# A different order of slots within an expert block of a mixture-of-experts step

## The chip, the cores and the metric

The kernel runs on one core of a Trainium2 chip. The metric is the device time of one execution in microseconds (us); the median of several runs is given. One further execution was recorded by the hardware profiler, and all rows shown below are of that one.

## The reference

One decoder layer is computed for 1040 prompt tokens (16 of them learned meta tokens) and 8 sample tokens, 1048 rows of 1024 numbers in float32: a mixer, then a mixture of experts, then a last norm. The mixer is not touched here. The mixture of experts is, cut to what matters:

```python
lg = h2 @ rg_w + rg_b;  gsel = top_k(lg, 1)            # one of 4 groups
le_g = (h2 @ re_w + re_b) of the chosen group          # 8 experts
ev, ei = top_k(le_g, 2)                                # two of the 8
wts = softmax(lg)[gsel] * softmax(ev)
for e in range(32):
    he = silu(h2 @ w_gate[e]) * (h2 @ w_up[e])         # 1024 -> 256
    out += combine[:, e] * (he @ w_down[e])            # 256 -> 1024
```

Each token is thus a row of two of the 32 experts, and 1048 x 2 = 2096 rows are to be worked on. The chosen experts depend on the data.

## The kernel before, in words

**Stages.** The mixer comes first. From about 500 us on, `route_parts` multiplies the mixer's result by the output weights (L2045) tile by tile (nine tiles of 128 tokens), and computes the router's choice of each tile on VectorE. From about 620 us on the expert stage runs, and from about 990 us on the last norm, which reads the experts' results back.

**How rows come to slots.** An expert has a block of C = 128 slots; one slot is one partition of the block's tile. In `place(t)` each token's *rank* within its expert is known: the number of tokens before it with the same expert. A token goes to the slot c for which `ic[c]` equals its rank:

```python
tt(in_slot[:, :, :], bc(rank[:, :, t], C), bc1(ic[:, :], 2), ALU.is_equal)
```

The product of this 0/1 matrix with the token numbers (`tabulate`, L1997) yields a table with a source row, a target row and a weight for each slot and expert. Slots without a token hold a row number out of bounds. `ic` is a constant of 128 columns, the same in each partition, that GpSimd writes with an iota in the function `gpsimd` (L1678). It counts 0, 1, 2, ..., so that the first n slots of a block with n tokens are filled. Ranks of 128 and more go to further blocks, at most 16 (`vector_extra`, L1931, compares with the same `ic`); here there are two such blocks.

**The expert stage.** Block e is worked on in these steps. GpSimd gathers the rows of the table from memory to the tile `xg`, 4 KB to a partition, with an indirect DMA (`gather`, L2088); rows out of bounds are left out. TensorE turns the tile (L2209). ScalarE and VectorE split the weights and the rows in a high and a low part (L2242, L2247, L2324, L2328), and TensorE makes three products of them for gate and up (L2273; two of the eight parts of the contraction, L2277, are made plain) and for down (L2349). VectorE and ScalarE weigh the result into `out`, and GpSimd scatters it with a second indirect DMA (L2200) to memory. Blocks 0 and 1 and the further blocks take plain products (L2256, L2315).

**Order.** TensorE does, for each block j: turn block j+2, turn the gated rows of j, gate and up of j+1, down of j. Three tiles and three sets of weights are in rotation. SyncE's queue loads the weights of block j+3: half of gate and up (L2110, 640 KB each of `w_gate` and `w_up`, both on one semaphore) when block j's first half is used, the other half (384 KB each) after the second, and down (L2127, 1024 KB) after block j's down products. The gather of block j+3 is issued when block j has been turned. All 128 slots are computed, filled or not.

Of the kernel before, what the change touches and what calls it, by code (L numbers as in the profile page):

```python
# [33 lines left out]
C = 128  # L34
# [1487 lines left out]
def route_parts(nc, m, s, b, io, sample):  # L1522
# [31 lines left out]
    ic = m.place("r_ic", [P, C])  # L1554
# [23 lines left out]
    part, base, isov = (m.place("r_" + name, [P, 2, T]) for name in ("part", "base", "isov"))  # L1578
# [27 lines left out]
    def h2_stored(eng):  # L1606
        eng.wait_ge(h2_out[0], 16 * 5)
        eng.wait_ge(h2_out[1], 16 * 4)
# [63 lines left out]
    def gpsimd(pool):  # L1672
        pool.wait_ge(b.ya_out[0], 16 * 2)
        it = nc.gpsimd.iota
        kw = dict(allow_small_or_imprecise_dtypes=True)
        it(iw[:, :], pattern=[[-1, 8]], base=8, channel_multiplier=0, **kw)  # L1676
        it(ib[:, :], pattern=[[1, OV]], base=1, channel_multiplier=0, **kw)
        it(ic[:, :], pattern=[[1, C]], base=0, channel_multiplier=0, **kw)  # L1678
        it(thr[:, :], pattern=[[C, PARTS - 1]], base=C, channel_multiplier=0, **kw)
        for k in range(2):  # L1680
            it(vals[:, 0, k, :], pattern=[[-P, T]], base=NOWHERE, channel_multiplier=-1, **kw)
            it(vals[:, 1, k, :], pattern=[[-P, T]], base=NOWHERE - k * TOK, channel_multiplier=-1, **kw)
        nc.gpsimd.memset(cum[0][:, :], 0.0).then_inc(iota, 1)
        sample.scale(pool)
        pool.wait_ge(prod, T)
        for k in range(SLOTS):
            nc.gpsimd.memset(b.xg[k][:, :], 0.0).then_inc(iota, 1)
        pool.wait_ge(iota, SLOTS + 1)
        h2_stored(pool)
        pool.wait_ge(b.rows_ok, 1)  # L1690
        for k in range(SLOTS):
            gather(pool, b, k, k)
# [385 lines left out]

    f = Shared()
    f.sync, f.gpsimd, f.scalar, f.vector, f.tensor, f.sync_more = sync, gpsimd, scalar, vector, tensor, sync_more  # L2080
    f.vector_extra, f.vector_tables, f.tensor_extra = vector_extra, vector_tables, tensor_extra
    f.idle_products, f.totals = idle_products, totals
# [3 lines left out]
def gather(pool, b, k, e, done=None):  # L2086

    pool.indirect_dma_start(b.xg[k][:, :], None, b.h2_dram,  # L2088
                            bass.IndirectOffsetOnAxis(ap=b.slot_rows[:, 0, e:e + 1].bitcast(U32), axis=0),
                            bounds_check=TOK - 1, oob_is_err=False).then_inc(b.gathered[k] if done is None else done, 16)  # L2090
# [767 lines left out]
```

## Time and profile before

| | |
|---|---|
| median of 3 runs | 1040.01 us (1036.04 to 1042.16) |
| the profiled execution | 1034.48 us, span 1032.7 us |
| TensorE busy | 974.1 us, 94% of the span |
| VectorE, ScalarE, GpSimd busy | 672.7, 503.6, 149.5 us |
| moved by DMA | 220.90 MB, of it 17.19 MB on GpSimd's queue |

The time of a run is a little longer than the span, which goes from the first to the last instruction. Busy shares are means over stages that differ; the chain of work that ended last tells what set the time of each stage. The share of the DMA engines is the time that packets took on the 16 engines of the core.

### The profile page before, as it was taken

The numbers are of one execution on the slowest core, as the hardware profiler recorded it, in microseconds if no ns is written. First come the engines' busy times: TensorE is split into PE (matmuls) and PEld (weight loads), VectorE is DVE, ScalarE is ACT, GpSimd is POOL, SyncE is SP. The second block draws the span as 40 slices with busy tenths as digits, with TensorE's granted clock in tenths as the row PEclk, the third lists the DMA queues.
The fourth block names the chain that finished last, engine by engine and source line by source line (L and its number), as shares of the span: only waits on it lengthen the run. The fifth ranks groups of instructions, "written<-read, shape, count | busy, mean of one in ns | idle before, by whom it ended". The sixth has DMA issues, their size and how long they took to land.

```text
span 1032.7 us, 15104 instructions
## 1 busy us (share of the span) xinstructions
PE 974.1 (94%) x5448; PEld 828.5 (80%) x5448; DVE 672.7 (65%) x1041; ACT 503.6 (49%) x891; POOL 149.5 (14%) x114
## 2 busy tenths in 40 slices
PE   5999999998999999999999988999999999999855
PEld 4889999998999999998888865677777777776422
DVE  7457676697434635356666667688887878787117
ACT  7487776433222332333223222577776766665115
POOL 2000000000000000000300011234434344442000
PEclk9999999999999999999999999999999999999988
DMA  7114667425753565458221159999999999995557
GB/s 243 45 42 126 164 156 198 119 83 170 207 157 109 155 167 135 142 166 264 79 82 59 48 225 294 375 356 372 379 367 349 354 346 360 347 393 213 187 212 313
DMA packets 127820, 220.90 MB, mean 214 GB/s; under 512 B 69516, under 2 KB 82374, under 8 KB 127758
## 3 DMA queue, kind: packets, MB, share of 16 engines
q1 hardware_dynamic: 115554, 194.20, 57.1%
q0 software_dynamic: 9792, 17.19, 4.5%
q10 hardware_dynamic: 2412, 8.68, 2.1%
q8 instruction: 38, 0.62, 0.2%
q14 instruction: 24, 0.20, 0.1%
HBM read 191.79 MB, written 46.72 MB: 231 GB/s over the span
## 4 chain that ended last, share of the span: by engine, by line
PE 75%; DMA 9%; DVE 9%; ACT 4%; issue 2%; SPq 0%; ACTq 0%; DVEq 0%; POOLq 0%
PE psum L1141 27%; PE psum L2045 10%; PE psum L2273 8%; DMA wd<-w_down 8%; PE psum L2349 5%; PE psum L2277 3%; PE psum L2256 2%; PE psum L1164 1%; PE psum L2209 1%; PE psum L2315 1%; PE psum L1980 1%; DVE it L953 1%; DVE xi L955 1%; ACT wd_hi L2324 1%; PE psum L1246 1%
## 5 line engine op out<-in xcount | busy, mean ns | idle before, releaser
L1141 PE MATMUL psum<-hh,wh 128*128 128x350 f32 x672 | 223.4, 332 | 3.9 <-issue 3.9
L1141 PE MATMUL psum<-hh,wl 128*128 128x350 f32 x672 | 217.9, 324 | 0.0
L1141 PE MATMUL psum<-hl,wh 128*128 128x350 f32 x672 | 217.3, 323 | 0.0
L1141 PEld LDWEIGHTS psum<-hh,wh 128*128 128x128 f32 x672 | 127.8, 190 | 5.3 <-issue 4.1
L1141 PEld LDWEIGHTS psum<-hl,wh 128*128 128x128 f32 x672 | 127.4, 190 | 0.9
L1141 PEld LDWEIGHTS psum<-hh,wl 128*128 128x128 f32 x672 | 127.2, 189 | 0.0
L2247 DVE TENSOR_TENSOR wgu_lo<-wgu,wgu_hi 128x1536 fp32r<-128x1536 f32 x60 | 104.9, 1749 | 0.5 <-ACT wgu_hi L2242 0.4
L2328 DVE TENSOR_TENSOR wd_lo<-wd,wd_hi 128x2048 fp32r<-128x2048 f32 x30 | 68.8, 2292 | 35.1 <-ACT wd_hi L2324 34.8
L2242 ACT ACTIVATE wgu_hi<-wgu 128x1536 fp32r<-128x1536 f32 x60 | 89.2, 1489 | 0.0
L2200 POOL DMA_INDIRECT expert_rows<-out,slot_rows x34 | 54.2, 1595 | 218.7 <-DVE out L2367 213.5
L2273 PE MATMUL psum<-wgu_hi,xgt_hi 128*128 128x512 f32 x180 | 85.3, 474 | 0.2
L2088 POOL DMA_INDIRECT xg<-h_rows,slot_rows x34 | 76.3, 2244 | 31.7 <-issue 17.6
L2324 ACT ACTIVATE wd_hi<-wd 128x2048 fp32r<-128x2048 f32 x30 | 57.6, 1918 | 41.2 <-DMA wd<-w_down 41.2
L855 DVE TENSOR_TENSOR wl<-wst,wh 128x1024 fp32r<-128x1024 f32 x28 | 34.3, 1225 | 64.4 <-ACT wh L629 64.3
L2273 PE MATMUL psum<-wgu_hi,xgt_lo 128*128 128x512 f32 x180 | 70.8, 394 | 0.0
L2273 PE MATMUL psum<-wgu_lo,xgt_hi 128*128 128x512 f32 x180 | 70.6, 392 | 0.0
L1676 POOL IOTA r_iw<- 128x8 f32 x1 | 0.1, 143 | 414.4 <-DMA mixer_rows<-th 414.4
L2277 PE MATMUL psum<-wgu,xgt_rest 128*128 128x512 f32 x120 | 56.3, 592 | 0.0
L897 DVE SCALAR_TENSOR_TENSOR acc<-raw,cqw,acc 128x1072 f32<-128x1072 f32 x36 | 48.0, 1333 | 0.9
L2045 PE MATMUL psum<-wo_hi,yt_hi 128*128 128x512 f32 (+1 forms) x144 | 47.8, 413 | 0.0
L2045 PE MATMUL psum<-wo_lo,yt_hi 128*128 128x512 f32 (+1 forms) x144 | 44.9, 393 | 0.0
L2273 PEld LDWEIGHTS psum<-wgu_hi,xgt_hi 128*128 128x128 f32 x180 | 33.9, 188 | 13.6 <-issue 8.0
(350 smaller groups left out, 1842.8 us busy)
## 6 DMA issues: line engine op xcount, KB each, us to landing
wd<-w_down SPq DMA_DIRECT2D x34, 1024.0 KB, 14.7
wgu<-w_gate SPq DMA_DIRECT2D x34, 640.0 KB, 6.0
wgu<-w_up SPq DMA_DIRECT2D x34, 640.0 KB, 13.4
wst<-w_in SPq DMA_DIRECT2D x28, 512.0 KB, 4.0
wgu<-w_gate SPq DMA_DIRECT2D x34, 384.0 KB, 6.5
wgu<-w_up SPq DMA_DIRECT2D x34, 384.0 KB, 14.6
ck<-qkv_rows SPq DMA_DIRECT2D x9, 702.0 KB
qkv_rows<-acc SPq DMA_DIRECT2D x12, 520.0 KB, 6.1
```

What stands on the lines that cost most here:

```text
L897: stt(ac[:, 0:QLEN], rw[:, q:q + QLEN], w[:, q:q + 1], ac[:, 0:QLEN], ALU.mult, ALU.add).then_inc(taps if q < KQ - 1 else conv_ok, 1)
L1141: ins = mm(ps[:, c, 0:ZC], w[:, kk, :], a[:, kk, c * ZC:(c + 1) * ZC], start=(kk == 0 and q == 0), stop=(kk == KD - 1 and q == 2))
L2045: ins = mm(ps[0:n, 2 * (t % 2) + c, :], y, w[:, c * 512:c * 512 + 512], start=(i == 0 and q == 0), stop=(i == KD - 1 and q == 2))
L2088: pool.indirect_dma_start(b.xg[k][:, :], None, b.h2_dram, bass.IndirectOffsetOnAxis(ap=b.slot_rows[:, 0, e:e + 1].bitcast(U32), axis=0), b ...
L2200: pool.indirect_dma_start(b.ye, bass.IndirectOffsetOnAxis(ap=b.slot_rows[:, 1, e:e + 1].bitcast(U32), axis=0), out[p][:, :], None, bounds_ ...
L2242: nc.scalar.activation(w_hi[x.p][h][:, :, :, :], half_of(b.slots[x.k][0], h), ACT.Copy).then_inc(w_hi_ok[h][x.p].sem, 1)
L2247: nc.vector.tensor_tensor(half_of(b.slots[x.k][1], h), half_of(b.slots[x.k][0], h), w_hi[x.p][h][:, :, :, :].bitcast(F32), ALU.subtract).t ...
L2273: ins = nc.tensor.matmul(gate_up_bank(x.p), a[:, c, :], w, start=(c == 0 and i == 0), stop=(c == KP - 1 and i == 2))
L2277: ins = nc.tensor.matmul(gate_up_bank(x.p), xt_rest[x.p][:, c, :], raw[:, :, kk, :], start=False, stop=False)
L2324: nc.scalar.activation(wd_hi[x.p][:, :, :], b.slots[x.k][2][:, :, :], ACT.Copy).then_inc(wd_hi_ok[x.p].sem, 1)
L2328: nc.vector.tensor_tensor(b.slots[x.k][3][:, :, :], b.slots[x.k][2][:, :, :], wd_hi[x.p][:, :, :].bitcast(F32), ALU.subtract).then_inc(wd_ ...
L2349: ins = nc.tensor.matmul(ps[0:C, 4 + 2 * x.p + c, :], h[x.p][:, f, :], w[:, f, c * 512:c * 512 + 512], start=(f == 0 and i == 0), stop=(f ...
```

## The change

The constant `ic` is written by four iotas of 32 columns each in place of one of 128. The column c = 32k + 4a + b, with k from 0 to 3, a from 0 to 7 and b from 0 to 3, gets the value 16 (k mod 2) + floor(k / 2) + 2a + 32b. This is a permutation of 0 to 127. The tokens of an expert thus go to other slots: rank 0 to slot 0, rank 1 to slot 64, rank 2 to slot 4, rank 32 to slot 1. The table, the gathers and the scatters follow from it, since they only use the table.

```diff
         it(iw[:, :], pattern=[[-1, 8]], base=8, channel_multiplier=0, **kw)
         it(ib[:, :], pattern=[[1, OV]], base=1, channel_multiplier=0, **kw)
-        it(ic[:, :], pattern=[[1, C]], base=0, channel_multiplier=0, **kw)
+
+        for k in range(4):
+            it(ic[:, 32 * k:32 * k + 32], pattern=[[2, 8], [32, 4]], base=16 * (k % 2) + k // 2, channel_multiplier=0, **kw)
         it(thr[:, :], pattern=[[C, PARTS - 1]], base=C, channel_multiplier=0, **kw)
```

## Rows read from the trace of the kernel before

**Rows 1.** The page: busy time of TensorE; queues with packets, MB, engines' share

```profile
PE 974.1 (94%) x5448; PEld 828.5 (80%) x5448; DVE 672.7 (65%) x1041; ACT 503.6 (49%) x891; POOL 149.5 (14%) x114
...
q1 hardware_dynamic: 115554, 194.20, 57.1%
q0 software_dynamic: 9792, 17.19, 4.5%
```

**Rows 2.** The chain that ended last, 560 to 1033 us: start, length, what

```profile
671.83 2.77 PE psum L2349 x12
...
779.24 2.77 PE psum L2349 x12
...
789.61 2.79 PE psum L2349 x12
792.56 15.98 DMA wd<-w_down
...
951.95 2.77 PE psum L2349 x12
...
969.56 7.15 PE psum L2256 x16
...
987.08 2.57 DMA expert_rows<-out,slot_rows
```

**Rows 3.** ScalarE's waits, 654 to 957 us: total, times, longest

```profile
ACT wd_hi L2324 <- DMA wd<-w_down: 41.2, 20, 2.9
```

**Rows 4.** Busy time by stretch; last three columns: TensorE clock, DMA share, GB/s

```profile
654.00:784.00 130.00, 129.87 (x582) 98.47 (x581) 109.17 (x105) 92.81 (x108) 50.74 (x26) 1.00 0.98 365
...
790.00:924.00 134.00, 131.60 (x583) 99.69 (x582) 108.93 (x105) 92.80 (x106) 55.05 (x26) 1.00 0.97 358
...
610.00:616.00 6.00, 3.04 (x23) 2.74 (x23) 4.62 (x24) 4.28 (x19) 0.00 (x0) 0.94 1.02 414
645.00:650.00 5.00, 5.00 (x34) 3.91 (x33) 0.84 (x2) 2.95 (x3) 0.00 (x0) 1.00 1.02 421
964.00:967.00 3.00, 3.00 (x8) 1.33 (x7) 0.00 (x0) 0.00 (x0) 0.00 (x0) 1.00 1.03 420
```

**Rows 5.** DMA issues, 654 to 674 us: KB each, median us to landing

```profile
wd<-w_down SPq DMA_DIRECT2D x2, 1024.0 KB, 7.2
wgu<-w_gate SPq DMA_DIRECT2D x2, 640.0 KB, 6.2
wgu<-w_up SPq DMA_DIRECT2D x2, 640.0 KB, 7.8
```

**Rows 6.** DMA issues, 774 to 794 us

```profile
wd<-w_down SPq DMA_DIRECT2D x2, 1024.0 KB, 16.1
wgu<-w_gate SPq DMA_DIRECT2D x2, 640.0 KB, 5.9
wgu<-w_up SPq DMA_DIRECT2D x2, 640.0 KB, 14.6
```

**Rows 7.** DMA issues, 955 to 984 us

```profile
wgu<-w_gate SPq DMA_DIRECT2D x1, 640.0 KB, 4.8
wgu<-w_up SPq DMA_DIRECT2D x1, 640.0 KB, 6.8
```

**Rows 8.** GpSimd in order of time, 423 to 504 us: start, length

```profile
423.00 0.24 POOL L1678 IOTA r_ic<- 128x128 f32 x1
423.19 0.14 POOL L1679 IOTA r_thr<- 128x8 f32 x1
423.28 0.15 POOL L1681 IOTA r_vals<- 128x9 f32 x1
...
503.70 1.61 POOL L1443 TENSOR_TENSOR s_in<-s_in,vals 128x512 f32<-128x512 f32 x1 [79.95 <-PE psum L1480]
```

**Rows 9.** VectorE in order of time, its first step of the router

```profile
491.53 0.25 DVE L1809 SCALAR_TENSOR_TENSOR lg<-psum,stat,rb 128x36 f32<-128x36 f32 x1 [6.63 <-PE psum L1980]
```

## The prediction

> **What bounds the kernel now.** I read the page first, then the chain of work that ended last over the last 480 us, then the waits in the expert stage, then the busy and transfer rates of single stretches, and last the DMA issues stretch by stretch. The page says TensorE is busy 94% of the span, and that two queues matter for this change: q1, which carries the weights, and q0, GpSimd's, which carries the gathers and scatters [rows 1]. The edit touches only which partition a row takes in the gathers and scatters, so the stage to understand is the expert stage, from about 654 to 954 us.
>
> Its chain has two parts. The rows of the chain at L2349 are the down products, one for each block. From 671.83 (block 2) to 779.24 (block 13) there are twelve of them in 11 equal steps, and nothing but TensorE stands between them: 107.41 / 11 = 9.765 us a block. That is TensorE's own pace. The next comes 10.37 us later, and from there to 951.95 (block 30) the chain runs again and again through a piece of about 16 us of "DMA wd<-w_down" [rows 2]. From block 13 to block 30 the 17 steps take 951.95 - 779.24 = 172.71 us, so 10.16 us each, where TensorE's pace would give 17 x 9.765 = 166.0. So the weights hold the second half of the stage up by 6.7 us. The waits agree on the place: ScalarE waits 41.2 us in 20 pieces for the down weights before it splits them, and most of that is slack of ScalarE itself, of which 6.7 us reach TensorE [rows 3].
>
> Why are the weights late? One block needs 3072 KB of weights (1024 down, 2 x 640 and 2 x 384 gate and up), which is 3.146 MB, and 17.19 MB / 34 = 0.506 MB of gathered and scattered rows [rows 1]: 3.65 MB in 9.765 us is 374 GB/s. The stage gets 365 GB/s in its first part and 358 in its second, with the DMA engines shown as 98% and 97% busy. Yet in three stretches in which nearly nothing but weights moved, the same engines gave 414, 421 and 420 GB/s [rows 4]. So 358 is no limit of the memory for such reads, and something in the mix makes full-looking engines slow.
>
> The issues of single stretches show what. The gate and the up half-load of 640 KB are issued one right after the other and count up the same semaphore. In 654 to 674 the first reaches its count after 6.2 us and the second after 7.8. In 774 to 794 the first takes 5.9 us, as ever, and the second 14.6; the down load has gone from 7.2 to 16.1 us [rows 5, 6]. Two transfers of one size in one queue can't land 9 us apart if all engines are equally far. But the two together make 32 counts, one for each engine and load, and "the first" is only the first 16 of them. If half of the engines are on time and have done both loads by 6 us, and the other half lags by 9 us, these are exactly the numbers. At the end of the stage, in the blocks of rows beyond 128, the pair lands after 4.8 and 6.8 us, so the same pair can be close [rows 7].
>
> And half the engines is what the kernel would load. 1048 tokens x 2 choices over 32 experts are 65.5 rows a block, and ranks are given to partitions in order from 0, so nearly all rows lie in partitions 0 to 63. An engine that serves a fixed group of partitions gets twice its share in the lower half and nearly nothing in the upper one. The sizes fit: 3.146 / 16 + 0.506 / 8 = 0.260 MB on an engine of the loaded half, over 10.16 us, is 25.6 GB/s, and 420 / 16 = 26.2 GB/s is what an engine does with weights alone [rows 1, 2, 4]. The lag is consistent too: from 7.2 to 16.1 us in 120 us, or 12.3 blocks, is 0.7 us a block, so that the loaded half needs some 10.2 to 10.5 us a block against TensorE's 9.765; after about a dozen blocks the three buffers' lead is used up, and that is where the chain changes [rows 2, 5, 6].
>
> The Trainium skill says the same of the place (DMA: Bandwidth & Descriptors, "The descriptor swizzle"): in a 128-partition transfer an engine serves eight fixed partitions, with bit 6 and bits 2 to 4 of the partition number choosing it, which puts partitions 0 to 63 on eight engines; after the change any 16 ranks in a row would by it fall on 16 engines. No row names an engine, so here that stays the skill's; what the rows show is that half of the counts lag.
>
> **The change part by part.** *The iota.* One IOTA of 128 columns (0.24 us) goes and four of 32 columns come. The short ones around it, of 8 to 16 columns, take 0.14 to 0.15 us, the long one 0.24, so four lie between 0.56 and 0.96 us busy, and the net cost on GpSimd is +0.3 to +0.7 us at 423 us. Behind them stand the other constants; the one who waits for these is VectorE, whose first use is at 491.53, 68 us later and after a wait for TensorE, and GpSimd itself then idles 79.95 us [rows 8, 9]. Cost 0; without that cover it would be at most 0.7 us.
>
> *The comparison with ic* (L1862, L1931) has the same shape with other values: 0. The products that build the table, the transposes, gate, up and down products work on all 128 rows in any case: 0.
>
> *The gathers and scatters.* The number of instructions, of rows, and of refused indices stays. What moves is the partition. Columns 32k+4a+b get rank 16(k mod 2) + floor(k/2) + 2a + 32b. So ranks 0 to 31 fill every fourth partition, 0 to 63 two of every four. Whatever fixed group of at least four neighbouring partitions an engine serves, it gets nearly the same number of rows. The load of each engine becomes 3.65 / 16 = 0.228 MB a block. At 26.2 GB/s that is 8.7 us, at the 25.6 worked out above 8.9; both lie 0.85 us or more under TensorE's 9.765. Then no backlog grows, the down load lands some 5 to 8 us after its issue instead of 16, the wait of 41.2 us at L2324 is gone, and the stage keeps TensorE's pace to its end. What is late next is TensorE itself, so nothing more than the 6.7 us can be had here.
>
> *Bounds.* Above: 6.7 us saved in full. Below: none, if the rows cost the engines their time wherever they lie: weights at 420 GB/s take 7.49 us, which leaves 10.16 - 7.49 = 2.67 us for 0.506 MB, or 190 GB/s [rows 2, 4]. Half of the engines, or slow rows on all: the sum alone can't tell the two apart, only the counts that split in two halves can [rows 6]. I take the full 6.7 for that reason.
>
> *Before and behind the stage.* The first gathers come sooner by perhaps 1 us, but the way to block 0's gated rows leads through VectorE's tables. The products of the last extra block start at 969.56, when the ones before end; they keep their distance. The last scatter takes 2.57 us, nearly all of it fixed [rows 2]: at most 0.5 us less, taken as 0.
>
> Here a rule of the skill speaks against the change. The Trainium skill (SBUF — State Buffer, "A bandwidth-pool intuition that's wrong (but worth ruling out)") puts the path from HBM to a core at about 358 GB/s and calls it nearly always the end-to-end bottleneck. By it a block's 3.65 MB need 10.2 us, spread or not, and the time would stay at 1040.0. The second half of the stage runs at 358, in its favour, but the rows with 414 to 421 GB/s are against it.
>
> **Sum.** -6.7 + 0 + 0 = -6.7 us. The profiled execution took 1034.48 us with a span of 1032.7; it would become 1027.8. The median of the runs is 1040.01 (1036.04 to 1042.16), 5.5 us above the profiled one; the same step there gives 1033.3, or 0.64% less. About 0.5%, 5.2 us, is what a measurement of this kernel can tell from no change.
>
> **The rivals.**
> *A common limit.* Reads, gathers and scatters share some 358 to 375 GB/s whatever the engines, or small rows are slow in themselves. For: 190 GB/s for the rows, above. Against: the halves of the counts that drift apart. Gain 0, so 1040.0; a mixture that leaves the period at 9.95 gives 17 x 0.2 = 3.4 us, 1036.6. Chance 0.21, nearly all of it within 0.5%. The skill's 358 GB/s, above, is this rival.
> *Rows dealt out to engines one by one* (partition modulo 16) and not by groups: this is the one that ends slower. Before, each engine would have its even share; after, ranks below 64 lie in partitions 0 and 1 of every four, which are 8 of 16 engines. Each of these would get 0.506 / 16 = 0.032 MB more, 1.2 us a block, and the period would be 10.16 + 1.2 = 11.4. From block 2 on, after a lead of some 6 us: 29 x (11.4 - 9.765) - 6 - 6.7 = 35 us more, about 1075. It decides from the point where the loaded engines need more than now. Against: with even shares now, no half of the counts could be early. Chance 0.03.
> *TensorE's clock.* With no pauses left TensorE is busy all through the stage, and the chip might grant less. In 654 to 784 it is busy 129.87 of 130 us, at a granted clock of 1.00, which is 2.4 GHz [rows 4], so full business there has not brought the lower level. If it came for 10 us, the stage would lose 5: 1038. Chance 0.04.
> *The edit has no effect on engines* (they take shares by the order of the descriptors that have data): 1040.0; counted with the common limit.
>
> **How the numbers follow.** The forecast has 0.70, with an own range of 1030.5 to 1036 from the spread of a median of few runs; the two rivals without a gain 0.25 together, the slower one 0.03, and 0.02 for more gain than I see. Of the forecast's 0.70 about 0.60 come out beyond 0.5%, since 6.7 us is close to 5.2; with the last 0.02 faster is 0.62. Within 0.5%: 0.10 + 0.21 + 0.02 = 0.33. Slower: 0.05. The range takes in the case without a gain: 1028.5 to 1040.
>
> **What would show it.** Right: L2349 in the chain steps by 9.77 us to block 30, at about 945.2 for that row instead of 951.95; no "DMA wd" pieces of 16 us in it; the wait at L2324 under 5 us; gate and up of a pair landing within 2 to 3 us of each other in every stretch; the down load at 5 to 8 us; some 370 GB/s at 90% DMA share. Wrong: pairs that still drift apart, or landings together but still at 12 us or more, would be the common limit. A granted clock under 1.00 between 654 and 950 would be the third rival.

## The result and the profile after

The changed kernel took 1032.34 us in the median of 7 runs (1028.33 to 1036.81), the kernel before 1037.29 us in 7 runs (1035.27 to 1042.16). The ratio is 0.9938, with a 95% interval of 0.9915 to 0.9961: 0.6% faster. (The two medians alone lie 4.95 us apart, 0.5%.) The profiled execution after took 1032.16 us, with a span of 1030.4 against 1032.7.

The chain of work that ended last, 560 to 1033 us (start, length, what). The lines of the code have moved by two, so L2351 is the L2349 of before:

```profile
676.55 2.77 PE psum L2351 x12
...
783.96 2.77 PE psum L2351 x12
...
793.72 2.77 PE psum L2351 x12
...
940.22 2.77 PE psum L2351 x12
...
949.10 2.79 PE psum L2351 x12
954.51 12.98 DMA wd<-w_down
...
985.05 2.34 DMA expert_rows<-out,slot_rows
```

From block 2 (676.55) to block 29 (940.22) lie 27 steps of 9.766 us without one exception, and no piece of waiting for weights stands between them; before, such pieces of 16 us began at 792 [rows 2]. From block 2 to block 30 the stage takes 949.10 - 676.55 = 272.55 us, before 951.95 - 671.83 = 280.12: 7.6 us less.

Busy time by stretch (last three columns: TensorE clock, DMA share, GB/s), then the DMA issues of 774 to 794 us (KB each, us to landing), then ScalarE's longest waits in 654 to 957 us:

```profile
654.00:784.00 130.00, 130.00 (x581) 97.92 (x580) 108.73 (x105) 89.86 (x104) 50.77 (x26) 1.00 0.99 364
790.00:924.00 134.00, 134.00 (x604) 102.85 (x603) 114.14 (x111) 95.25 (x109) 53.51 (x28) 1.00 1.01 373
```

```profile
wd<-w_down SPq DMA_DIRECT2D x2, 1024.0 KB, 9.3
wgu<-w_gate SPq DMA_DIRECT2D x2, 640.0 KB, 5.9
wgu<-w_up SPq DMA_DIRECT2D x2, 640.0 KB, 7.9
```

```profile
ACT thx L2286 <- PE psum L2275: 48.5, 30, 3.3
...
ACT out L2362 <- PE psum L2351: 37.9, 30, 3.6
```

TensorE is busy in all of the 134 us from 790 to 924, where it was 131.60 [rows 4]. The gate and the up load land 2.0 us apart, where it was 8.7 [rows 6]. ScalarE's wait for the down weights, 41.2 us before [rows 3], has no row any more; ScalarE now waits for TensorE.

The profile as a whole is only 2.3 us shorter, though. The iotas on GpSimd, which wait for a mixer result, start at 426.36 us after and at 422.81 before: 3.5 us are lost before the first changed instruction. From there to block 2 it is 250.19 against 249.02, 1.2 more. The stage gives 7.6, the tail takes 0.8 (from block 30's down products to the last scatter 35.95 us, before 35.13), and the end gives 0.3. What stands ahead of the iotas can't be the change's doing; the rows show where the two executions part there. The stretches of before, and then of after (the third last column is TensorE's granted clock):

```profile
52.00:78.00 26.00, 23.43 (x141) 21.64 (x141) 14.25 (x23) 22.13 (x37) 0.00 (x0) 1.00 0.12 41
640.00:660.00 20.00, 20.00 (x85) 12.68 (x84) 8.14 (x11) 8.35 (x9) 2.71 (x2) 0.94 1.00 401
```

```profile
52.00:78.00 26.00, 23.43 (x126) 20.96 (x125) 13.79 (x22) 18.87 (x32) 0.00 (x0) 0.87 0.07 21
640.00:660.00 20.00, 18.17 (x71) 10.93 (x72) 6.37 (x14) 4.60 (x7) 0.00 (x0) 0.83 0.97 382
```

From 52 to 78 us TensorE was granted 0.87 of full speed after and 1.00 before, and 26 x 0.13 = 3.4 us is nearly all of the 3.5. From 640 to 660 us it was 0.83 against 0.94, which is enough for the 1.2. Such stretches differ between executions of one kernel: from 52 to 78 us the change was granted 0.87 in two profiles and 0.93 in a third (again2), as was in_order. So the medians, and not the two profiles, are the measure of the change.

### The profile page after: what moved, and what is told of

Its sections match the earlier page's. It is cut to its first block, busy times and chain, and to the rows that moved or that the text cites. A ratio compares the mean times of both kernels' runs of the same rounds, so it can differ in the third digit from the quotient of the medians.

```text
span 1030.4 us, 15107 instructions
## 1 busy us (share of the span) xinstructions
PE 975.8 (95%) x5448; PEld 832.6 (81%) x5448; DVE 674.7 (65%) x1041; ACT 502.1 (49%) x891; POOL 141.4 (14%) x117
## 3 DMA queue, kind: packets, MB, share of 16 engines
q0 software_dynamic: 9792, 17.19, 4.8%
## 4 chain that ended last, share of the span: by engine, by line
PE 85%; DVE 8%; DMA 3%; ACT 2%; issue 1%; SPq 0%; DVEq 0%; ACTq 0%; POOLq 0%
PE psum L1141 27%; PE psum L2275 12%; PE psum L2047 10%; PE psum L2351 8%; PE psum L2279 5%; PE psum L2211 3%; PE psum L1164 2%; PE psum L2258 2%; PE psum L1982 1%; PE psum L2317 1%; DMA wd<-w_down 1%; DVE it L953 1%; DVE xi L955 1%; PE psum L1246 1%; DVE acc L897 1%
## 5 line engine op out<-in xcount | busy, mean ns | idle before, releaser
L2090 POOL DMA_INDIRECT xg<-h_rows,slot_rows x34 | 67.6, 1988 | 32.0 <-PE psum L2211 11.5
L2369 DVE TENSOR_SCALAR out<-psum,slot_w 128x512 f32<-128x512 f32 x34 | 25.5, 751 | 52.5 <-PE psum L2351 42.7
L2286 ACT ACTIVATE thx<-psum 128x256 f32<-128x256 f32 x34 | 13.1, 384 | 76.6 <-PE psum L2275 48.5
```

Of the source, the lines that this page charges most:

```text
L2090: pool.indirect_dma_start(b.xg[k][:, :], None, b.h2_dram, bass.IndirectOffsetOnAxis(ap=b.slot_rows[:, 0, e:e + 1].bitcast(U32), axis=0), b ...
```

## The experiments

All ratios are to runs of the kernel before on the same chip, with 95% intervals.

**The change once more, and its slots undone.** The first is the kernel after as it is.

> The change once more, beside the next three on one chip. All theories: some 6 us (0.6%) below the kernel before, no 16 us piece of waiting for the down weights in the chain, gate and up of a pair landing some 2 us apart.

The second keeps the four iotas and gives back the old values:

```diff
-            it(ic[:, 32 * k:32 * k + 32], pattern=[[2, 8], [32, 4]], base=16 * (k % 2) + k // 2, ...)
+            it(ic[:, 32 * k:32 * k + 32], pattern=[[4, 8], [1, 4]], base=32 * k, ...)
```

> Four iotas as in the change, but with the values 0 to 127 in order, so the slots are those of before. My theory (the partitions of the rows count, the iotas are hidden): same time as before, ratio 0.998 to 1.002, the up load lands 14 to 15 us after its issue in the second half of the stage. Rival (something about the program itself, such as a different alignment of code or clock, made the gain): ratio near 0.994.

Measured: 0.989 (0.9867 to 0.9912) for the change, and 0.9988 (0.9967 to 1.0008) in order. In order, the up load lands after 14.7 us in 790 to 924, gate after 6.0, ScalarE waits 40.8 us for the down weights (654 to 957 us), and block 2 to block 30 takes 953.67 - 673.81 = 279.86 us. All the gain is in the order of the slots.

**Which partitions count?** Two other permutations part the ways in which an engine could be tied to partitions. In the first, ranks 0 to 63 fill the partitions whose bit 2 is 0; in the second, those whose bit 5 is 0.

```diff
+            it(ic[...], pattern=[[2, 4], [64, 2], [16, 4]], base=8 * (k % 2) + k // 2, ...)   # bit2_last
+            it(ic[...], pattern=[[2, 8], [16, 4]], base=64 * (k % 2) + k // 2, ...)           # bit5_last
```

> Ranks 0 to 63 in the partitions whose bit 2 is 0 (0 to 3, 8 to 11, ...), spread evenly over every run of eight neighbouring partitions and over both halves. If an engine serves two groups of four partitions chosen by bits 2 to 4 and 6, as the Trainium skill has it, eight engines again get nearly all rows: ratio 0.998 to 1.002, up load at 14 us, 16 us waits in the chain. If an engine serves eight neighbouring partitions, or if it is enough that the rows lie over all 128 partitions: even load, ratio near 0.994, up load near 8 us.

> Ranks 0 to 63 in the partitions whose bit 5 is 0 (0 to 31 and 64 to 95), the other half of the partitions nearly empty. If bits 2 to 4 and 6 choose the engine, all 16 engines have the same number of rows as with the change: ratio near 0.994, up load near 8 us. If an engine serves eight neighbouring partitions, or if all 128 partitions must be used: ratio 0.998 to 1.002, up load at 14 us.

DMA issues of 790 to 924 us, with bit 2 last, and then with bit 5 last:

```profile
wd<-w_down SPq DMA_DIRECT2D x13, 1024.0 KB, 15.4
wgu<-w_gate SPq DMA_DIRECT2D x14, 640.0 KB, 6.2
wgu<-w_up SPq DMA_DIRECT2D x14, 640.0 KB, 13.8
```

```profile
wd<-w_down SPq DMA_DIRECT2D x13, 1024.0 KB, 9.0
wgu<-w_gate SPq DMA_DIRECT2D x14, 640.0 KB, 6.0
wgu<-w_up SPq DMA_DIRECT2D x14, 640.0 KB, 8.0
```

With bit 5 last half of the partitions are nearly empty, and yet the pair lands 2.0 us apart, the stage takes 272.54 us (677.26 to 949.80), and the ratio is 0.9901 (0.9878 to 0.9924), that of the change. With bit 2 last the rows lie in all parts of the 128 partitions, 4 in every 8, and yet the pair drifts 7.6 us apart, and the waits for down weights are back: 41.3 us at ScalarE, and pieces like this one in the chain (900 to 1000 us):

```profile
914.80 2.79 PE psum L2350 x12
917.60 16.93 DMA wd<-w_down
...
945.95 2.77 PE psum L2350 x12
...
954.82 2.79 PE psum L2350 x12
```

So neither "it is enough that all 128 partitions are used" nor "an engine serves eight neighbours" holds. The runs speak for four of the seven bits: with ranks 0 to 63 on one value of bit 6 (slots in order) or of bit 2 the pair drifts apart, with one value of bit 5 or of bit 1 (the change, whose ranks 0 to 63 lie in partitions with bit 1 at 0) it does not. Bits 0, 3 and 4 were not parted. All this agrees with the Trainium skill's rule (DMA: Bandwidth & Descriptors, "The descriptor swizzle"): bit 6 and bits 2 to 4 choose the engine, and bit 5 and bits 0 and 1 do not. The profile has no engine numbers, so the rule is seen here by its effect alone.

One number missed its expectation. With bit 2 last the ratio is 0.9937 (0.9914 to 0.996) and not 1.00. The stage takes 278.05 us (676.77 to 954.82), 2 less than before. That accounts for 0.2% of the 0.6%; the rest was not found in the stage (see what stays open). As to the 2 us: eight engines carry most rows in both kernels, but not equally. By that rule and the routing of these inputs, worked out with the reference, the fullest engine has 7.6 rows a block and transfer with the slots in order (the one of partitions 0 to 3 and 32 to 35 is full in every block of 36 tokens or more) and 6.9 with bit 2 last. The next experiment measures this.

**The transfers laid bare.** In the kernel itself TensorE's pace hides most of what the transfers need. So a third of the gate and up products of the split parts is left out, and with it VectorE's subtraction that feeds it, while every transfer stays:

```diff
-                for i, (a, w) in enumerate(((hi_x, hi_w), (hi_x, lo_w), (lo_x, hi_w))):
+                for i, (a, w) in enumerate(((hi_x, hi_w), (hi_x, lo_w))):
...
-                if x.parts:
-                    turned_low(dve, x)
+                pass
```

The waits for the result of that subtraction go with it.

> Slots as before, but TensorE's third product of gate and up (low rows by high weights) is left out, and with it VectorE's subtraction that makes the low rows; all transfers stay. TensorE then needs some 7.4 us a block, VectorE 7.3, so that the transfers alone set the pace from early on. Skewed engines: 10.1 to 10.2 us a block, the time within 5 us of the kernel before, although a quarter of TensorE's work is gone. If the 10.16 us of the kernel before came from an interplay with TensorE, the block would get faster.

> The same cut with the slots of the change. Skewed engines: the load of the fullest engine falls from some 0.259 to 0.233 MB a block, so 9.0 to 9.2 us a block, and 25 us or more less than light_before. Common limit (all transfers share one rate wherever the rows lie): the same pace as light_before, 10.1 us a block.

> The same cut with ranks 0 to 63 in the partitions whose bit 2 is 0. By the fullest engine (6.9 rows a block and transfer instead of 7.6 before, worked out from the routing): 0.254 MB, 9.9 to 10.0 us a block, some 4 to 6 us below light_before and 20 above light_after. If only the split in halves counted: as light_before.

ScalarE's split of the down weights comes once a block, so its rows in order of time (start, length) give the pace. Two rows of each kernel, 19 blocks apart: slots in order, those of the change, bit 2 last.

```profile
693.46 1.92 ACT L2323 ACTIVATE wd_hi<-wd 128x2048 fp32r<-128x2048 f32 x1 [2.10 <-DMA wd<-w_down]
...
890.12 1.92 ACT L2323 ACTIVATE wd_hi<-wd 128x2048 fp32r<-128x2048 f32 x1 [3.22 <-DMA wd<-w_down]
```

```profile
697.30 1.92 ACT L2325 ACTIVATE wd_hi<-wd 128x2048 fp32r<-128x2048 f32 x1
...
862.71 1.92 ACT L2325 ACTIVATE wd_hi<-wd 128x2048 fp32r<-128x2048 f32 x1 [0.89 <-DMA wd<-w_down]
```

```profile
692.55 1.92 ACT L2324 ACTIVATE wd_hi<-wd 128x2048 fp32r<-128x2048 f32 x1 [2.59 <-DMA wd<-w_down]
...
881.31 1.92 ACT L2324 ACTIVATE wd_hi<-wd 128x2048 fp32r<-128x2048 f32 x1 [2.58 <-DMA wd<-w_down]
```

| slots | us a block | median, us | ratio | fullest engine by the rule, MB a block |
|---|---|---|---|---|
| in order | 196.66 / 19 = 10.35 | 1035.74 | 0.997 (0.9941 to 0.9999) | 0.197 + 2 x 7.6 x 0.0041 = 0.259 |
| bit 2 last | 188.76 / 19 = 9.93 | 1029.63 | 0.992 (0.9896 to 0.9944) | 0.253 |
| the change's | 165.41 / 19 = 8.71 | 998.82 | 0.9618 (0.9574 to 0.9662) | 0.233 |

The weights alone are 3.146 / 16 = 0.197 MB on an engine, and 0.0041 MB is a row. The change's slots have 4.5 rows for the 7.6 and take 0.197 + 2 x 4.5 x 0.0041 = 0.233.

With the slots in order TensorE's smaller work brings 3 us; the blocks don't get faster with less for TensorE to do (10.35 us here, and (951.95 - 789.61) / 16 = 10.15 in the kernel before [rows 2]), so the transfers and not an interplay with TensorE set that pace. With the change's slots the same cut brings some 33 us. TensorE alone would need 8.36 us there, as the next experiment shows, and the 19 steps hold one of 8.36 us before ScalarE's waits begin, so that 8.71 (8.73 without that step) is an upper bound of what the transfers need. And these transfers, rows and all, run at this rate (stretches of light_after):

```profile
700.00:760.00 60.00, 59.17 (x263) 44.12 (x262) 51.38 (x49) 47.86 (x55) 25.61 (x15) 1.00 1.03 417
780.00:880.00 100.00, 99.40 (x441) 74.03 (x440) 86.63 (x84) 80.40 (x93) 43.22 (x24) 1.00 1.03 415
```

415 GB/s with gathers and scatters in it is the rate that weights alone had before (414 to 421) [rows 4]. The common limit of 358 GB/s is refuted, and so are rows that are slow in themselves. The order of the three follows the fullest engine: the eight loaded engines carry nearly the same mean in the first two lines (6.6 and 6.7 rows by the same count), but the pace differs by 0.4 us. The rates by the table (0.259 / 10.35 = 25.0 GB/s, 25.5, 26.8) don't agree to better than 7%, so the fullest engine alone is a good guide and no exact law. Two expectations were missed: 8.71 us is below the 9.0 to 9.2 that I gave light_after, and light_bit2 is 31 us above light_after and not 20. A third premise was wrong too: the cut takes 9.77 - 8.36 = 1.4 us of TensorE's block, 14% and not a quarter.

**Fewer bytes in place of a better order.** In `gather`, `bounds_check` is 0 in place of TOK - 1, so that every row but row 0 is left out and the experts work on zeros (the results are not those of the layer), once on the light kernel with the change's slots, once on the kernel before.

> light_after, and the gathers take no rows: their bound is 0, so every index above 0 is left out and the experts work on zeros; instructions, indices and scatters stay. By bytes on even engines: 0.215 MB, 8.4 us a block, 0.6 to 0.8 us below light_after. If a gathered row costs the engines much more than its bytes (row reads slow in themselves, 2.67 us a block for gathers and scatters together), it is 1.3 us or more below light_after.

This one told nothing of what it was for. Its blocks take (853.33 - 694.49) / 19 = 8.36 us with TensorE busy 100.00 of 100 us, so TensorE, which I had put at 7.4 us, set the pace, and the transfers lay below it. It gives an upper bound only, and a ratio of 0.9528 (0.9483 to 0.9574).

> Slots as before, full TensorE work, but the gathers take no rows (bound 0; the experts work on zeros, the scatters stay). The fullest engine's load falls from some 0.259 to 0.228 MB a block, under TensorE's 9.77 us at 25.5 GB/s. If the bytes on the fullest engine set the pace before: all steps of the stage at 9.77 us and the ratio of the change, 0.989 to 0.994, with the skewed slots. If the order of slots did something else: the ratio stays at 0.998 to 1.002.

Ratio 0.9914 (0.9887 to 0.9941). The chain of this kernel, with the slots in order:

```profile
672.93 2.77 PE psum L2349 x12
...
936.60 2.77 PE psum L2349 x12
945.47 2.79 PE psum L2349 x12
```

Block 2 to block 30 takes 272.54 us, to 0.01 the time of the change. Taking the gathered bytes off the loaded engines does as much as spreading them; both only bring the transfers under TensorE's pace.

**The tail, and the change a third time.** In the profile after, TensorE has a new wait in the blocks of rows beyond 128 (TensorE in order of time, 955 to 972 us; the window cuts the 16 products to 11):

```profile
967.53 4.99 PE L2258 MATMUL psum<-wgu,xgt 128*128 128x512 f32 x11 [0.79 <-DMA wd<-w_down]
```

There gate, up and down loads count up one semaphore, and gate and up wait for all. `tail_split` gives the down load its own:

```diff
+    more_d = s.again_pair("v_d")
...
-                    load_down(sp, b, io, e, more_k[p], more_w[p].sem)
+                    load_down(sp, b, io, e, more_k[p], more_d[p].sem)
...
-                    pe.wait_ge(more_w[p].sem, more_w[p].at(80 * (n + 1)))
+                    pe.wait_ge(more_w[p].sem, more_w[p].at(64 * (n + 1)))
...
+                    pe.wait_ge(more_d[p].sem, more_d[p].at(16 * (n + 1)))
                     down(pe, more[p], p, n, more_k[p])
```

> The change a third time, since the two ratios so far, 0.994 and 0.989, stand apart. From the profiles the stage gives 7.6 us and the tail takes 0.8 back: ratio 0.993 to 0.994. If the 0.989 was not chance but more than the stage, it comes again: 0.988 to 0.990.

> The change, and in the blocks of rows beyond 128 the down weights get a semaphore of their own, so that gate and up no longer wait for them. If the wait of 0.79 us of TensorE in the profile after is the down load's, it goes: 0.5 to 0.8 us less than the change, too little to be timed, but the wait before the last block's gate and up products is gone from the profile. Rival (the rows or gate and up themselves are late): the wait stays, with another name.

TensorE in order of time, 954 to 974 us:

```profile
959.73 13.90 PE L2259 MATMUL psum<-wgu,xgt 128*128 128x512 f32 x32
```

With the semaphore of its own all 32 products run in one piece, so the down load was what the last block waited for. The ratio is 0.9922 (0.9896 to 0.9949), and 0.9911 (0.9875 to 0.9946) for the change measured beside it: 0.8 us can't be told by time. The change itself has now had 0.9938, 0.989 and 0.9911. The stage took 272.55, 272.55 and 272.54 us in the three profiles, so the spread comes from elsewhere (see the spread of the ratios, below).

## Why the prediction was right, point by point

*The place and the cause.* Right, and shown. Half of the engines lagged because of the partitions of the rows: the change, bit5_last and in_order show it from one side, bit2_last from the other, where rows lie in all 128 partitions and the lag stays. How many engines lag is read from the split of the counts; no row names them. What was worth most in the profile was two like loads on one semaphore that landed 9 us apart [rows 6].

*The size.* Forecast 6.7 us, 0.64%, and 1033.3; measured 0.62%, 1032.34. That both come so close is in part luck: 1033.3 was counted from a median of 1040.01 in 3 runs, which 7 runs put at 1037.29, and the ratios of the same change in the two later measurements are 1.1% and 0.9%. In the stage itself it was 7.6. The term that was mis-sized is TensorE's own time for the 17 steps from block 13 to block 30, which I put at 17 x 9.765 = 166.0. The last step turns no further block and takes 949.10 - 940.22 = 8.88 us, so it is 16 x 9.765 + 8.88 = 165.1, and 172.7 - 165.1 = 7.6. The 0.9 us that were missed there and the 0.8 us that the tail took back cancel by chance. A smaller slip: 17.19 MB over 34 blocks is 0.506 MB, but by the routing the two further blocks hold only 29 of the 2096 rows, so one of the 32 moves 0.53 MB; nothing hangs on it.

*The tail.* "They keep their distance" was wrong. In the profile before, the last block's down load (SyncE's queue, then the DMA issues of 955 to 984 us) landed about when TensorE came free:

```profile
957.37 0.38 SPq L2127 DMA_DIRECT2D wd<-w_down  x1
```

```profile
wd<-w_down SPq DMA_DIRECT2D x1, 1024.0 KB, 12.1
```

957.37 + 12.1 = 969.5, beside 969.56 [rows 2]. After, it is issued at 954.51 and takes 12.98, to 967.49, where TensorE was free at 966.74. Its issue keeps its distance to TensorE, but it lands 0.9 us later after it. The issues of the last two blocks lie closer together after, 952.62 - 943.75 = 8.87 us against 955.47 - 945.74 = 9.73 (their first loads), which may be why; it was not tested. tail_split shows that it was the down load.

*The iotas.* Four took 0.64 us in all (the forecast was 0.56 to 0.96), hidden at 426 us. in_order shows no cost, with 0.9988 (0.9967 to 1.0008), but a cost of 0.4 us, 0.04%, it could not have told.

*The load after the change.* I worked out 8.7 us a block at the rate of weights alone and 8.9 at the other. light_after measured 8.71. Of the 10.35 - 8.71 = 1.64 us a block that the transfers gained, TensorE's pace of 9.766 lets only a part through, and that part only once the lead of the buffers is used up: 7.6 us of 28 x 1.64 = 46. Most of the change's gain is not in its time but in room.

*The down load's landing.* Forecast 5 to 8 us, measured 9.3 (9.0 over 790 to 924 us). The forecast has no sum for it and stays near the 7.2 us of the stage's start [rows 5]. In the profile after, the loads of two blocks overlap in the queue; see the last section.

*The signs.* The pairs, the wait at L2324 and the 373 GB/s came as forecast. Two did not: the row of block 30 stands at 949.10 and not at 945.2, since block 2 came 4.7 us later, and the DMA share is 1.01 and not 90%. 370 GB/s over the 414 to 421 of weights alone is 0.89, but the shown share does not follow the rate: 373 GB/s are shown at 1.01 after, 358 at 0.97 before, and 415 at 1.03 in light_after.

*The rivals.* The common limit: refuted by 415 GB/s in light_after. Rows dealt out by modulo: refuted, since the change would have been slower. TensorE's clock: 1.00 in both stretches of the stage, with TensorE busy without a gap. The three measurements of the change (the highest end of an interval is 0.9961) are all below 1, and in two of them the whole interval is beyond the 0.5% that I gave as what can be told (0.9912 and 0.9946).

*The spread of the ratios.* The stage and the tail explain 6.8 of 1038 us, hence 0.9934; 0.989 is further from 1, with its whole interval (to 0.9912). The record has the mean granted clock of TensorE over each execution, and the time follows it: over 108 runs of the kernel before, the change and the variants with TensorE's full work, a run is 7.5 us longer for each 0.01 less of clock (one slope fitted to all, a level for each kernel and measurement). The runs of the change had a mean clock of 0.9796, 0.9837 and 0.9837. At 0.98 they come to 1032.1, 1032.0 and 1032.1 us, and those of the kernel before, in the three later measurements, to 1039.4 to 1039.8. So at one clock the change is worth 7.6 us, with an error of about 1, and most of what parts the three ratios is the clock that was granted. It is a fit and no experiment: no kernel here was made to vary the clock.

**What stays open.** With bit 2 last the same fit gives 1035.7, 4 us less than before, of which the stage shows 2. Why the fullest engine's rate differs by 7% between the kernels, and why a block takes 10.35 us in light_before and 10.15 in the kernel before, is open. So is what lags in the lagging half: the engine itself, or the path by which it reaches its partitions.

## What to carry to other kernels

A gather or scatter whose tile is filled in partition order can load a part of the DMA engines only, even if each transfer spans 128 partitions: here half, with 65 rows in 128 slots. Spread the filled slots over the groups that the engines serve, which needs no more than another constant in the comparison that deals out the slots. When transfers share engines with a full-width stream, count the bytes of the fullest engine, not the mean; and to see what a stream needs that compute hides, make the compute smaller and read the pace, and see first that the smaller compute is out of the way: in light_nogather it was not.

Before you compare two kernels that differ by under 1%, look at the granted clock of the runs.

## What the runs showed that I had not expected

The DMA share says little of how much more could be moved, and the rate moves much within a block. In the profile after, just after the 640 KB loads of a block were issued (840.65 and 841.08 us), and in the second half of the same block:

```profile
841.50:844.00 2.50, 2.50 (x12) 2.04 (x11) 2.47 (x3) 1.41 (x2) 0.48 (x1) 1.00 1.02 318
845.50:849.50 4.00, 4.00 (x21) 3.04 (x20) 3.99 (x5) 3.82 (x6) 2.11 (x2) 1.00 1.02 380
```

It is 318 GB/s against 380, with a DMA share shown as 1.02 in both, while light_after holds 415 to 417 at 1.03. In the kernel before the share was 0.97 with half of the engines ahead of their work [rows 4]. The 318 are not those of an empty queue. This is the down load issued before them (SyncE's queue, then the DMA issues of 835 to 837 us):

```profile
835.59 0.38 SPq L2129 DMA_DIRECT2D wd<-w_down  x1
```

```profile
wd<-w_down SPq DMA_DIRECT2D x1, 1024.0 KB, 8.8
```

It landed at 835.59 + 8.8 = 844.4, so it was still on its way when the next loads had been out for 3.7 us. That the loads of two blocks overlap may also be why a down load takes some 9 us in a kernel without a lag. Why the rate is lower there was not tried.

TensorE's granted clock differed where the same work was done: 0.91 of full speed from 700 to 760 us in light_before, where it was busy 52.90 of 60 us, but 1.00 in light_bit2, busy 51.89 of 60, and 1.00 in light_before itself from 780 to 880, busy 85.67 of 100. In light_before the transfers set the pace, so this cost nothing that the runs show; the 0.87 from 52 to 78 us in the profile after cost about 3.4 us.
